# Where the upward projections stand in the fused middle phase of a two-layer transformer kernel

## The chip, the cores and the metric

The kernel runs on one core of a Trainium2 chip, as one program. The metric is the device time of one execution in microseconds (us); for the kernel before it is the median of three runs. One further execution was taken by the hardware profiler, and every row below is from that one.

## The reference

A first block (a gated delta rule beside stick-breaking attention) is followed by a second one. The part that matters here is the end of the first block and the beginning of the second, on 1024 tokens of 1024 features, all in fp32:

```python
# end of the first block
return x + jnp.einsum('bsd,de->bse', merged.astype(x.dtype), w_out)
# beginning of the second block
h = rms_norm(x, attn_norm_g[i])
z = h @ w_in[i]                                   # 1024 x 1952
q  = rms_norm(q_lat,  q_lat_g)  @ w_uq            # z[:, 0:256]   -> 768 columns
kv = rms_norm(kv_lat, kv_lat_g) @ w_ukv           # z[:, 256:384] -> 1024 columns
```

q_lat and kv_lat are the first 384 columns of z. After this come two kinds of attention, which read q, kv and the other columns of z, then an output projection, a gated convolutional feed-forward layer and an embedding gate.

## The kernel before

The kernel is a row of phases. A phase allocates its buffers and semaphores, gives each of five engines its instruction stream, and ends with a barrier over all engines. The changed one is the phase named "trunk", from about 1280 to 1583 us of the span; the phase behind it is "attend".

Each fp32 product is made of three matrix products: every operand is split into a high part and a rest, and high x high, high x rest and rest x high are added in PSUM. So weights are loaded raw from HBM and split: ScalarE copies the raw tile into the high part (`split_hi`, L2943), VectorE subtracts for the rest (`split_lo`, L2948).

`WeightRing` (L2906) does this for the whole phase. Its list of chunks is numbered: 0 and 1 are the two column halves of w_out, 2 to 5 the four column chunks of the second block's w_in (512, 512, 512 and 416 columns), 6 holds w_uq and w_ukv. A chunk has two halves h. There are two slots of split weights (chunk i uses slot i % 2) and one raw buffer per half. One ring step, for chunk i and half h, is: on ScalarE, wait until the half is loaded and until chunk i - 2 has been used to its end (`ended`, L2941), then `split_hi`; on VectorE, `split_lo`; on SP, wait for that `split_lo`, then issue the load of half h of chunk i + 1 (L2935).

The stages of the phase walk over eight token tiles m of 128 tokens each:

- `OutProject` and the `Norm` stages: the output projection of the first block with its residual, the norm, and the turn into feature-major tiles.
- `InProject` (L3254): for each column chunk i and token tile m, 24 products into one PSUM bank (L2987 to L2989), one copy of the bank to an output buffer, one store to HBM (z).
- `LatentScale` and `LatentTurn`: the norm of the 384 latent columns and their turn, spread over the first column chunk and the start of the second.
- `UpProject` (L3432): for each token tile four pieces, q0 and q1 (384 columns, two feature tiles, 6 products each) and kv0 and kv1 (512 columns, one feature tile, 3 products each), at L3488 to L3490, each with its own bank, copy and store (q_mla, kv_mla).

All copies go through `Outputs` (L3218): four output buffers and four PSUM banks, both taken in a fixed rotation in the order of the plan. A copy waits until its bank is filled and until the store of four pieces earlier has landed (`stored`); then it frees the bank. For input tiles ScalarE copies the even m and VectorE the odd ones; for upward pieces ScalarE copies q0 and kv0, VectorE q1 and kv1 (L3239, L3241). SP issues each store when its copy is done (L3246), waiting for the copies one after another.

The order is written out by hand in `trunk_plan` (L3504), a list of stage numbers. Every engine runs the steps of all stages in the order of this list, its own part of each; so a step of SP that waits holds up all stores that stand behind it in the list. In the plan a ring step stands behind the token tiles m = 2 and m = 4 of each of the six chunks; the eight upward steps stand at the very end, with no ring step among them. SP's last work in the phase is the wait for all stores, in the upward stage (`wait_stored`).

Of the kernel before, what the change touches and what calls it, by code (L numbers as in the profile page):

```python
# [17 lines left out]
TT = SEQ // P  # L18
# [5 lines left out]
class Phase:  # L24


    def __init__(self, nc, name):
        self.nc, self.name, self.stack, self.sems = nc, name, ExitStack(), []
# [562 lines left out]
class Heads:  # L591
# [93 lines left out]
    def part(self, tensor, j, s):  # L685
        if 4 * s < self.nh:
            return tensor[:, 4 * s:4 * s + 4, :], 0
        return tensor[:, 4 * s - self.nh:4 * s - self.nh + 4, j % TT * P:(j % TT + 1) * P], 1
# [19 lines left out]
class StickAttention:  # L708
# [34 lines left out]
    def keys(self, u):  # L743
        return (self.units[u][0] + 1) * P
# [9 lines left out]
    def sync(self, sp):  # L754
        def store(j):
            sp.wait_ge(self.o_out, j + 1)
            sp.dma_start(self.out[j * P:(j + 1) * P, :], self.o_sb[:]).then_inc(self.stored, 16)

        self.prep.load(sp, 0)
        self.prep.load_gains(sp)  # L760
        sp.dma_start(self.v_sb[:], self.v.rearrange("(k p) d -> p k d", p=P)).then_inc(self.v_in, 16)
        self.prep.load(sp, 1)
        for i in range(self.steps()):
            if self.next_tile(i, 0) is not None:
                self.prep.load(sp, self.next_tile(i, 0))
            if i >= len(self.units):
                yield
                continue
            j, h = self.units[i]
            if h == 5 and j:  # L770
                store(j - 1)
            yield
        store(TT - 1)
        sp.wait_ge(self.stored, 16 * TT)

    def gpsimd(self, pool):
        self.prep.begin_inverse(pool)
        self.nc.gpsimd.memset(self.zero[:], 0.0).then_inc(self.zeroed, 1)
        for j in range(2):
            self.prep.inverses(pool, j)  # L780
        for i in range(self.steps()):
            if self.next_tile(i, 5) is not None:
                self.prep.inverses(pool, self.next_tile(i, 5))
            yield
# [2198 lines left out]
def token_products(nc, out, hi, lo, tok, ring, i, kt):  # L2983

    for k in range(kt):
        w_hi, w_lo = (w[:, k % (kt // 2)] for w in ring.weights(i, k // (kt // 2)))
        nc.tensor.matmul(out, hi[:, k, tok], w_hi, start=(k == 0), stop=False)  # L2987
        nc.tensor.matmul(out, hi[:, k, tok], w_lo, start=False, stop=False)  # L2988
        last = nc.tensor.matmul(out, lo[:, k, tok], w_hi, start=False, stop=(k == kt - 1))  # L2989
    return last  # L2990


def tile_of(m):
    return slice(m * P, (m + 1) * P)
# [259 lines left out]
class InProject:  # L3254


    def __init__(self, o, outputs, widths, target, first_chunk):
        self.o, self.outputs, self.widths, self.target, self.first_chunk = o, outputs, widths, target, first_chunk
        self.base = [sum(widths[0:i]) for i in range(len(widths))]
        self.latent = None  # L3260
        for i in range(len(widths)):
            o.ring.ended[first_chunk + i] = (o.acc, ("in", i, TT - 1))

    def walk(self):
        return [(i, m) for i in range(len(self.widths)) for m in range(TT)]
# [5 lines left out]
    def sync(self, sp):  # L3271
        for i, m in self.walk():
            self.outputs.store(sp, ("in", i, m), self.target[tile_of(m), self.base[i]:self.base[i] + self.widths[i]], self.widths[i])
            yield

    def gpsimd(self, pool):
        return iter(())
# [16 lines left out]
    def tensor(self, pe):  # L3294
        o = self.o
        for i, m in self.walk():
            key, chunk = ("in", i, m), self.first_chunk + i
            if m == 0:
                for h in range(2):
                    o.ring.wait_split(pe, chunk, h)  # L3300
            if i == 0:
                o.wait_parts(pe, m)
            o.acc.wait_free(pe, key)
            last = token_products(o.nc, o.acc.tile(key)[:, 0:self.widths[i]], o.hi, o.lo, tile_of(m), o.ring, chunk, 8)
            o.acc.fill(last, key)
            yield
# [125 lines left out]
class UpProject:  # L3432
# [4 lines left out]

    def __init__(self, l, q, kv, chunk):
        self.l, self.targets, self.chunk = l, (q, kv), chunk

    def keys(self, m):
        return [("up", m, x) for x in range(len(self.PIECES))]
# [4 lines left out]
    def sync(self, sp):  # L3447
        l = self.l

        def store(m):  # L3450
            for key, (which, c0, w) in zip(self.keys(m), self.PIECES):
                l.outputs.store(sp, key, self.targets[which][tile_of(m), c0:c0 + w], w)

        for m in range(TT):
            store(m)
            yield
        l.outputs.wait_stored(sp)

    def gpsimd(self, pool):
        return iter(())  # L3460
# [34 lines left out]
def take_in_order(plan, stages):  # L3495

    seen = [0] * len(stages)
    for which in plan:
        for slots, key in stages[which].takes(seen[which]):
            slots.take(key)  # L3500
        seen[which] += 1


def trunk_plan():  # L3504

    ring, out, scale, turn, into, l_scale, l_turn, up = range(8)
    plan = [ring, ring]
    for m in range(TT):
        plan += [out, scale]
        plan += [ring] * (m in (2, 4))  # L3510
    for m in range(TT):
        plan += [out]
        plan += [turn] * (m >= 2) + [scale]
        plan += [ring] * (m in (2, 4))
    for i in range(4):
        for m in range(TT):
            if i == 0 and m in (1, 2):
                plan += [turn]
            if 3 <= TT * i + m < 3 + TT:
                plan += [l_turn]  # L3520
            plan += [into]
            if i == 0:
                plan += [l_scale]
            plan += [ring] * (m in (2, 4))
    plan += [up] * TT
    return plan


# [264 lines left out]
def two_blocks(nc, a, out):  # L3793

    def scratch(name, *shape):
        return nc.dram_tensor(f"scratch_{name}", list(shape), F32, kind="Internal").ap()
# [6 lines left out]
    def two_chunks(w0, w1, width):  # L3803

        return lambda c, h: (w0, w1)[h][:, ds(c * width, width)].rearrange("(k p) n -> p k n", p=P)
# [4 lines left out]
    def parts(stack, name, kt):  # L3810
        return (stack.enter_context(nc.sbuf_tensor(f"{name}_hi", [P, kt, SEQ], F32R)),
                stack.enter_context(nc.sbuf_tensor(f"{name}_lo", [P, kt, SEQ], F32R)))

    with ExitStack() as ctx:
# [31 lines left out]
        x1, z2 = scratch("x1", SEQ, D), scratch("z2", SEQ, 1952)  # L3846
        q_mla, kv_mla = scratch("q_mla", SEQ, MLA_H * QK), scratch("kv_mla", SEQ, MLA_H * (NOPE + MLA_V))
        with ExitStack() as stage:
            m_hi, m_lo = parts(stage, "merged", 8)
            with ExitStack() as inner:  # L3850
                hi, lo = parts(inner, "branches", 8)
                gather_branches(nc, "gather1", o_a, o_b, z_a, qkv_z_b[:, 1536:], a["dn_out_gain"], hi, lo, ident)
                project_merge(nc, "merge", hi, lo, two_chunks(a["w_up_a"], a["w_up_b"], 256), gates, m_hi, m_lo)
            with Phase(nc, "trunk") as ph:
                in_widths = [HALF, HALF, HALF, 1952 - 3 * HALF]
                columns_of = [(a["w_out"], 0, HALF), (a["w_out"], HALF, HALF)]
                columns_of += [(a["w_in_2"], i * HALF, w) for i, w in enumerate(in_widths)]
                chunked = [[(4, w, source[h * HALF:(h + 1) * HALF, c0:c0 + w]) for h in range(2)] for source, c0, w in columns_of]
                ring = WeightRing(ph, nc, chunked + [[(2, 768, a["w_uq_2"]), (1, 1024, a["w_ukv_2"])]])
                acc, turn = Slots(ph, "acc", 4, [P, HALF]), Slots(ph, "turn", 1, [P, 8, P])  # L3860
                outputs = Outputs(ph, nc, acc)
                o = OutNorm(ph, nc, m_hi, m_lo, a["x"], x1, a["attn_norm_g_2"], ring, acc, turn, c)
                l = Latent(ph, o, outputs, [a["q_lat_norm_g_2"], a["kv_lat_norm_g_2"]])
                with ExitStack() as own:
                    o.place_inputs(Own(ph, own))
                l.hi, l.lo = (ph.sb(f"latent_{n}", [P, 3, SEQ], F32R) for n in ("hi", "lo"))
                into = InProject(o, outputs, in_widths, z2, 2)
                into.latent = l
                stages = [ring, OutProject(o), NormScale(o), NormTurn(o), into, LatentScale(l), LatentTurn(l),
                          UpProject(l, q_mla, kv_mla, 6)]  # L3870
                plan = trunk_plan()
                take_in_order(plan, stages)
                run_stages(ph, stages, plan)
# [60 lines left out]
```

## Time and profile before

| | us |
|---|---|
| median of 3 runs | 3100.68 (3097.73 to 3104.68) |
| profiled execution | 3099.98 |
| its span | 3097.9 |
| TensorE busy (PE) | 2658.8 (86%) |
| VectorE busy (DVE) | 1276.2 (41%) |
| ScalarE busy (ACT) | 987.7 (32%) |
| mean granted TensorE clock | 0.93 of full speed |

A row of the profile's timeline has the start and the duration in us, the engine, the line of the kernel, the operation and its tiles, and in brackets the idle time before it with what ended that idle time. PE is TensorE, PEld its weight loads, DVE VectorE, ACT ScalarE, POOL GpSimd, SP or SPq the queue that issues the DMAs. The profiled duration of a matrix product is modelled and overlaps the next one, so the pace of TensorE is read from starts. The granted clock is 1.00 at the 2.4 GHz level and 0.50 at the 1.2 GHz level.

### The profile page before, as it was taken

Reading aid. Unit: us, or ns where it says so; the run is one execution under the profiler, and the core shown is the slowest. Engines: PE = TensorE matmul, PEld = TensorE weight load, DVE = VectorE, ACT = ScalarE, POOL = GpSimd, SP = SyncE. Lnnn points to the kernel's source line nnn. Section 1 sums busy time; section 2 is a strip of 40 time slices with the busy share of each in tenths; the row PEclk is TensorE's granted clock in tenths of the full one; section 3 lists DMA queues with packets and bytes.
Section 4 is the critical chain, followed back from the end, with each engine's and each line's share of the span. In section 5 each row is a group of like instructions: output and inputs, shape, how many; then the busy total and the mean of one; then the engine's idle time right before and its main releaser. Section 6 shows DMA issues by size and latency. Waiting matters only on the chain. (4 is left out here: it accounts for less than half of the span.)

```text
span 3097.9 us, 39044 instructions
## 1 busy us (share of the span) xinstructions
PE 2658.8 (86%) x15182; PEld 2295.4 (74%) x15182; DVE 1276.2 (41%) x1831; ACT 987.7 (32%) x1582; POOL 240.3 (8%) x309
## 2 busy tenths in 40 slices
PE   5979999995998928799958889495999999799569
PEld 4859999995887827688946677484888888678469
DVE  4533444433655544342137666513333332333332
ACT  3323222212554531122126666402222221222321
POOL 0002222211000000010013221000000000000000
PEclk9989999997999969899978999797999999899779
DMA  2322212103221133432161110233222221454432
GB/s 89 109 75 77 72 49 59 54 30 99 79 72 38 38 120 136 160 101 94 67 215 48 33 49 16 91 123 103 61 81 61 81 74 55 139 186 142 156 98 93
DMA packets 253786, 272.77 MB, mean 88 GB/s; under 512 B 55716, under 2 KB 190500, under 8 KB 253640
## 3 DMA queue, kind: packets, MB, share of 16 engines
q1 hardware_dynamic: 252584, 268.68, 27.6%
q8 instruction: 98, 1.61, 0.2%
q10 hardware_dynamic: 1056, 2.10, 0.2%
q14 instruction: 48, 0.39, 0.0%
HBM read 193.50 MB, written 77.22 MB: 87 GB/s over the span
## 5 line engine op out<-in xcount | busy, mean ns | idle before, releaser
L395 PE MATMUL ffn_up_acc<-xn_hi,ffn_w_hi 128*128 128x512 f32 x704 | 217.7, 391 | 3.6 <-PEq L39 3.6
L395 PE MATMUL ffn_up_acc<-xn_hi,ffn_w_lo 128*128 128x512 f32 x704 | 217.2, 390 | 0.0
L395 PE MATMUL ffn_up_acc<-xn_lo,ffn_w_hi 128*128 128x512 f32 x704 | 217.2, 390 | 0.0
L1717 PE MATMUL delta_acc<-delta_w_hi,xn_hi 128*128 128x256 f32 x640 | 192.0, 300 | 2.9 <-DVE delta_w_lo L1671 2.9
L1719 PE MATMUL delta_acc<-delta_w_hi,xn_lo 128*128 128x256 f32 x640 | 181.4, 284 | 0.0
L1718 PE MATMUL delta_acc<-delta_w_lo,xn_hi 128*128 128x256 f32 x640 | 181.4, 283 | 0.0
L2987 PE MATMUL trunk_acc<-trunk_ring_hi,merged_hi 128*128 128x512 f32 (+1 forms) x384 | 149.6, 390 | 19.6 <-DVE trunk_ring_lo L2948 19.6
L2107 PE MATMUL ffn_down_acc<-ffn_down_hi 128*128 128x512 f32 x352 | 139.1, 395 | 25.2 <-DVE ffn_down_lo L2092 25.2
L395 PEld LDWEIGHTS ffn_up_acc<-xn_hi,ffn_w_hi 128*128 128x128 f32 x704 | 132.6, 188 | 31.2 <-DMA gather_o<-scratch_o_diff 3.8
L395 PEld LDWEIGHTS ffn_up_acc<-xn_lo,ffn_w_hi 128*128 128x128 f32 x704 | 132.7, 188 | 27.6
L395 PEld LDWEIGHTS ffn_up_acc<-xn_hi,ffn_w_lo 128*128 128x128 f32 x704 | 132.5, 188 | 27.6
L2988 PE MATMUL trunk_acc<-trunk_ring_lo,merged_hi 128*128 128x512 f32 (+1 forms) x384 | 148.0, 385 | 0.0
L2989 PE MATMUL trunk_acc<-trunk_ring_hi,merged_lo 128*128 128x512 f32 (+1 forms) x384 | 147.7, 385 | 0.0
L2092 DVE TENSOR_TENSOR ffn_down_lo<-ffn_down_raw,ffn_down_hi 128x1536 fp32r<-128x1536 f32 x44 | 77.3, 1759 | 165.3 <-ACT ffn_down_hi L2073 165.3
L849 DVE TENSOR_TENSOR_SCAN stick_keep<-stick_keep,stick_zero 128x127 f32<-128x127 f32 (+7 forms) x64 | 86.7, 1355 | 134.8 <-ACT stick_keep L800 134.7
L2108 PE MATMUL ffn_down_acc<-ffn_down_lo,ffn_down_hi 128*128 128x512 f32 x352 | 138.5, 394 | 0.0
L2109 PE MATMUL ffn_down_acc<-ffn_down_hi,ffn_down_lo 128*128 128x512 f32 x352 | 138.4, 393 | 0.0
L1717 PEld LDWEIGHTS delta_acc<-delta_w_hi,xn_hi 128*128 128x128 f32 x640 | 122.4, 191 | 8.9 <-issue 5.5
L2073 ACT ACTIVATE ffn_down_hi<-ffn_down_raw 128x1536 fp32r<-128x1536 f32 x44 | 65.4, 1487 | 189.0 <-PE ffn_down_acc L2109 175.0
L261 PE MATMUL norm_t<-ident,norm_xn 128*128 128x128 f32 x192 | 46.0, 420 | 92.4 <-DVE norm_xn L238 92.4
L1718 PEld LDWEIGHTS delta_acc<-delta_w_lo,xn_hi 128*128 128x128 f32 x640 | 122.5, 191 | 0.0
L1719 PEld LDWEIGHTS delta_acc<-delta_w_hi,xn_lo 128*128 128x128 f32 x640 | 122.3, 191 | 0.0
(401 smaller groups left out, 6294.5 us busy)
## 6 DMA issues: line engine op xcount, KB each, us to landing
ffn_down_raw<-scratch_act_t SPq DMA_DIRECT2D x44, 512.0 KB, 3.5
ffn_w_raw<-in_w_gate SPq DMA_DIRECT2D x22, 512.0 KB, 4.5
ffn_w_raw<-in_w_up SPq DMA_DIRECT2D x22, 512.0 KB, 5.7
scratch_act_t<-ffn_up_silu SPq DMA_DIRECT2D x22, 512.0 KB, 3.2
ffn_down_raw<-in_w_down SPq DMA_DIRECT2D x44, 256.0 KB, 3.7
delta_w_raw<-in_w_in SPq DMA_DIRECT2D x20, 512.0 KB, 3.9
scratch_projected<-delta_out SPq DMA_DIRECT2D x80, 128.0 KB, 1.7
stick_g_raw<-in_w_in SPq DMA_DIRECT2D x16, 512.0 KB, 4.7
```

The costliest lines, as they stand in the source:

```text
L395: last = nc.tensor.matmul(out[:, cols], weight[:, k, ch], part[:, k, cols], start=(k == 0 and first), stop=(k == kt - 1 and weight is w_lo))
L849: nc.vector.tensor_tensor_scan(back, back, self.zero[:].to_broadcast([P, n - 1]), 1.0, ALU.mult, ALU.add).then_inc(self.scanned, 1)
L1717: nc.tensor.matmul(acc, self.hi[:, k, tok], w_hi, start=(k == 0), stop=False, skip_group_check=True)
L1718: nc.tensor.matmul(acc, self.hi[:, k, tok], w_lo, start=False, stop=False, skip_group_check=True)
L1719: last = nc.tensor.matmul(acc, self.lo[:, k, tok], w_hi, start=False, stop=(k == self.kt - 1), skip_group_check=True)
L2092: nc.vector.tensor_tensor(lo[s][:], raw[s][:], hi[s][:].bitcast(F32), ALU.subtract).then_inc(lo_done[s], 1)
L2107: nc.tensor.matmul(acc[m][:], hi[s][:, tok], w_hi, start=start, stop=False, skip_group_check=True)
L2108: nc.tensor.matmul(acc[m][:], hi[s][:, tok], w_lo, start=False, stop=False, skip_group_check=True)
L2109: last = nc.tensor.matmul(acc[m][:], lo[s][:, tok], w_hi, start=False, stop=stop, skip_group_check=True)
L2987: nc.tensor.matmul(out, hi[:, k, tok], w_hi, start=(k == 0), stop=False)
L2988: nc.tensor.matmul(out, hi[:, k, tok], w_lo, start=False, stop=False)
L2989: last = nc.tensor.matmul(out, lo[:, k, tok], w_hi, start=False, stop=(k == kt - 1))
```

## The change

The list of ring chunks gets the upward weights as number 4, between the second and third column chunks, which with the fourth are now 5 and 6. `InProject` takes a list of chunk numbers, [2, 3, 5, 6], in place of the first number, and `UpProject` takes 4 and tells the ring when it has ended. In the plan the eight upward steps stand behind the last token tile of the second column chunk. As the last column chunk now has nothing to split ahead, its two ring steps are gone, and two ring steps stand in the upward stage, behind its token tiles 2 and 4. There they split the third column chunk and load the fourth. The wait for all stores moves to the input stage. The numbers of products, copies, stores and loads are the same.

```diff
@@ class InProject
-    def __init__(self, o, outputs, widths, target, first_chunk):
+    def __init__(self, o, outputs, widths, target, chunks):
...
         for i in range(len(widths)):
-            o.ring.ended[first_chunk + i] = (o.acc, ("in", i, TT - 1))
+            o.ring.ended[chunks[i]] = (o.acc, ("in", i, TT - 1))
...
             self.outputs.store(sp, ("in", i, m), ...
             yield
+        self.outputs.wait_stored(sp)
...
-            key, chunk = ("in", i, m), self.first_chunk + i
+            key, chunk = ("in", i, m), self.chunks[i]
@@ class UpProject
         self.l, self.targets, self.chunk = l, (q, kv), chunk
+        l.o.ring.ended[chunk] = (l.o.acc, self.keys(TT - 1)[-1])
...
-        l.outputs.wait_stored(sp)
@@ trunk_plan
             plan += [into]
             if i == 0:
                 plan += [l_scale]
-            plan += [ring] * (m in (2, 4))
-    plan += [up] * TT
+            plan += [ring] * (m in (2, 4) and i < 3)
+        if i == 1:
+            for m in range(TT):
+                plan += [up] + [ring] * (m in (2, 4))
     return plan
@@ two_blocks
-                ring = WeightRing(ph, nc, chunked + [[(2, 768, a["w_uq_2"]), (1, 1024, a["w_ukv_2"])]])
+                chunked[4:4] = [[(2, 768, a["w_uq_2"]), (1, 1024, a["w_ukv_2"])]]
+                ring = WeightRing(ph, nc, chunked)
...
-                into = InProject(o, outputs, in_widths, z2, 2)
+                into = InProject(o, outputs, in_widths, z2, [2, 3, 5, 6])
...
-                          UpProject(l, q_mla, kv_mla, 6)]
+                          UpProject(l, q_mla, kv_mla, 4)]
```

## Rows read from the trace of the kernel before

**Rows 1.** Busy time by stretch: from:to, its length, then busy us of each engine.
```profile
core 0: us, PE busy (x) PEld busy (x) DVE busy (x) ACT busy (x) POOL busy (x), PEclk, DMA share, GB/s
1424.00:1550.00 126.00, 126.00 (x594) 110.06 (x593) 22.52 (x26) 17.81 (x25) 1.08 (x3) 1.00 0.20 72
1551.00:1579.00 28.00, 27.91 (x143) 25.33 (x141) 9.74 (x17) 8.75 (x16) 0.00 (x0) 1.00 0.67 245
```

**Rows 2.** Timeline of TensorE in the upward stage: start us, duration us, engine, line.
```profile
1550.58 0.34 PE L3488 MATMUL trunk_acc<-trunk_ring_hi,trunk_latent_hi 128*128 128x384 f32 x1
...
1554.11 0.34 PE L3488 MATMUL trunk_acc<-trunk_ring_hi,trunk_latent_hi 128*128 128x384 f32 x1
```

**Rows 3.** Waits in the upward stage: us in total, times, longest.
```profile
ACT trunk_out L3239 <- DMA scratch_kv_mla<-trunk_out: 1.3, 1, 1.3
```

**Rows 4.** Timeline of ScalarE and VectorE in the second column chunk.
```profile
1444.05 0.60 ACT L3239 ACTIVATE trunk_out<-trunk_acc 128x512 f32<-128x512 f32 x1 [5.03 <-PE trunk_acc L2989]
1444.55 1.91 ACT L2943 ACTIVATE trunk_ring_hi<-trunk_ring_raw 128x2048 fp32r<-128x2048 f32 x1
1454.88 0.60 ACT L3239 ACTIVATE trunk_out<-trunk_acc 128x512 f32<-128x512 f32 x1 [8.43 <-PE trunk_acc L2989]
...
1446.49 2.29 DVE L2948 TENSOR_TENSOR trunk_ring_lo<-trunk_ring_raw,trunk_ring_hi 128x2048 fp32r<-128x2048 f32 x1 [6.88 <-ACT trunk_ring_hi L2943]
```

**Rows 5.** DMA issues with us to landing: load, store behind it, upward stores, 1024 KB loads.
```profile
L2935 SPq DMA_DIRECT2D trunk_ring_raw<-in_w_in x1: 383/383/383, 1448.8 to 1448.8; - x1
DMA to landing us min/median/max: 4.8/4.8/4.8
...
L3246 SPq DMA_DIRECT2D scratch_z<-trunk_out x1: 320/320/320, 1450.2 to 1450.2; - x1
DMA to landing us min/median/max: 4.1/4.1/4.1
...
L3246 SPq DMA_DIRECT2D scratch_kv_mla<-trunk_out x8: 319/319/320, 1554.2 to 1565.6; - x8
L3246 SPq DMA_DIRECT2D scratch_q_mla<-trunk_out x8: 319/319/319, 1555.9 to 1567.6; - x8
DMA to landing us min/median/max: 1.8/2.0/2.9
...
trunk_ring_raw<-in_w_in SPq DMA_DIRECT2D x2, 1024.0 KB, 5.7
```

**Rows 6.** Timeline of the copies of the first upward token tile.
```profile
1551.84 0.49 ACT L3239 ACTIVATE trunk_out<-trunk_acc 128x384 f32<-128x384 f32 x1 [5.05 <-PE trunk_acc L3490]
1553.60 0.60 ACT L3239 ACTIVATE trunk_out<-trunk_acc 128x512 f32<-128x512 f32 x1 [1.27 <-PE trunk_acc L3490]
...
1552.90 0.56 DVE L3241 COPY trunk_out<-trunk_acc 128x384 f32<-128x384 f32 x1 [1.53 <-PE trunk_acc L3490]
```

**Rows 7.** Busy time by stretch: TensorE standing still, and the start of the next phase.
```profile
46.00:49.00 3.00, 0.00 (x0) 0.00 (x0) 1.23 (x1) 0.69 (x1) 0.14 (x2) 1.00 0.00 0
1800.00:1802.00 2.00, 0.08 (x1) 0.08 (x2) 1.93 (x10) 0.59 (x2) 0.34 (x1) 1.00 0.19 66
1802.00:1805.00 3.00, 3.00 (x17) 3.00 (x18) 1.39 (x2) 0.98 (x3) 0.00 (x0) 0.57 0.79 203
...
1584.00:1642.00 58.00, 22.71 (x82) 16.68 (x83) 27.08 (x97) 17.58 (x46) 13.55 (x22) 0.50 0.59 169
```

**Rows 8.** Timeline of the end of the phase, with a copy of 416 columns.
```profile
1550.78 0.59 DVE L3241 COPY trunk_out<-trunk_acc 128x416 f32<-128x416 f32 x1 [8.42 <-PE trunk_acc L2989]
...
1578.87 1.11 SPq L3246 DMA_DIRECT2D scratch_kv_mla<-trunk_out  x2
1578.94 0.69 DVE L3241 COPY trunk_out<-trunk_acc 128x512 f32<-128x512 f32 x1 [0.84 <-PE trunk_acc L3490]
...
1582.92 0.34 SPq L2169 DMA_DIRECT2D attend_bias_table<-in_rel_bias  x1
```

More of the change, by code:

```diff
@@ L3254 @@
 class InProject:
-    def __init__(self, o, outputs, widths, target, first_chunk):
-        self.o, self.outputs, self.widths, self.target, self.first_chunk = o, outputs, widths, target, first_chunk
+    def __init__(self, o, outputs, widths, target, chunks):
+        self.o, self.outputs, self.widths, self.target, self.chunks = o, outputs, widths, target, chunks
         self.base = [sum(widths[0:i]) for i in range(len(widths))]
```

## The prediction

> **What bounds the kernel now.** I read the page's shares first, then the stretches of the fused phase one by one, because a share over 3098 us says nothing about one stage. In the stretches [rows 1] the reader is to see that TensorE is busy 126.00 us of 126.00 in the input projection and 27.91 of 28.00 in the upward projection that now ends the phase, at a granted clock of 1.00, while ScalarE and VectorE have 8.75 and 9.74 us of work in the latter. So TensorE's own stream sets the length of both, and an order of the same products gains nothing by itself: there is no idle TensorE time between them for the moved stage to fill. What differs is the rate of the small jobs around the products. An input tile has 24 products, one copy and one store, and takes 5.4 us (ScalarE copies every other one, 10.83 us apart [rows 2]); an upward token tile has 18 products, 12 of them 384 wide, takes 3.53 us (first product at 1550.58, the next token tile's at 1554.11 [rows 3]), and has four copies and four stores. The stage has 8 such tiles: 8 x 3.53 = 28.2 us. Its DMA share is 0.67 at 245 GB/s, against 0.20 at 72 GB/s before it [rows 1]. The upward stage is thus bound by TensorE with the output buffers close behind: one copy already waited 1.3 us for an earlier store [rows 4].
>
> **The change, part by part.** Time t below runs from the first upward product; a piece is one of q0, q1 (384 wide), kv0, kv1 (512 wide). Order of work only: no product, copy, store or load is added or removed.
>
> *Products moved.* Their 28.2 us are spent in the middle instead of at the end. Nil.
>
> *Ring steps that now fall inside the upward stage.* Before, the last ring steps stood in the fourth column chunk, and none in the upward stage. Now the stage's token tiles 2 and 4 are each followed by one: ScalarE splits half of the third column chunk's weights (128x2048, 1.91 us), VectorE makes the rest (2.29 us) [rows 2], and SP, which waits for VectorE there, issues the load of the fourth chunk's half (832 KB). Among the input tiles such a step is free, 24 products (5.4 us) standing for one copy and one store. In the upward stage four pieces pass in 3.53 us. What is queued behind it: on SP the stores of the next token tile, on ScalarE its q0 copy, on VectorE its q1 copy; for the stores wait the copies four pieces later (four output buffers), and for these TensorE (four PSUM banks).
>
> How much later a store behind such a load lands is in the trace: the 832 KB load issued at 1448.8 landed 4.8 us later, at 1453.6, and the 256 KB store issued at 1450.2 took 4.1 us, to 1454.3, so 0.7 us after the load [rows 5]; upward stores without a load ahead take 1.8 to 2.9, median 2.0 [rows 5]. So I take stores as served in order behind the load. The bytes behind it go at 245 GB/s / 0.67 = 366 GB/s [rows 1]: 0.72 us for 256 KB, 0.54 us for 192 KB.
>
> The chain, step by step. The first kv0 copy starts 3.02 us after the stage's first product and takes 0.60 [rows 3, 6]; that of tile 2 ends at t = 7.06 + 3.02 + 0.60 = 10.7. Split 1.91, to 12.6. Rest of the split 2.29, to 14.9. SP issues the load, which lands 4.8 later, at 19.7. Stores of tile 3 behind it: q0 to 20.3, q1 to 20.8, kv0 to 21.5 (0.54, 0.54, 0.72). The kv0 copy of tile 4 needs that last one's buffer: 0.60, to 22.2. On ScalarE the second split follows: 1.91, then 2.29 on VectorE, to 26.4. Second load lands at 31.2; q0 store of tile 5 at 31.8; the q0 copy of tile 6 (0.49) frees its bank at 32.3; TensorE starts tile 7 and ends at 32.3 + 3.53 = 35.9. Without ring steps the end is 28.2, so TensorE stands still for **7.7 us**. In pieces: 0.4 ahead of q1 of tile 4 (its bank waits for a VectorE copy behind the split), 2.9 ahead of tile 5, some 0.2 and 1.3 in tile 6, 2.9 ahead of tile 7.
>
> Bounds of it: if the stores pass the load and land 2.0 after their issue, only the busy VectorE counts. The first VectorE step ends at 14.9 instead of the copy at 13.4 (0.4 of TensorE) and the second at 23.0, its q1 copy to 23.6 where TensorE wanted the bank at 22.5 (1.1): 1.4 us. If each load takes 5.7 us, as the 1024 KB ones of the ring [rows 5], 7.7 + 2 x 0.9 = 9.5 us. I take 7.7, the nearest row being a load of the same size with a store behind it.
>
> The Trainium skill bears on this. In "DMA: Bandwidth & Descriptors", section "Queues, rings and completion order", it says that descriptors are consumed in ring order but that completion is not first-in first-out per issuing engine. By the order of consumption the sum is 7.7 us; by free completion it would go toward 1.4. The one row with a store behind a load sides with order.
>
> *Clock.* TensorE's stops of 2.9 us come twice. The trace has a stop of 3 us with the clock staying at 1.00 (46 to 49 us), and one of 2 us after which it was 0.57 over the next three (1802 to 1805, so 2.6 us of those at half, the 1.2 GHz level) [rows 7]. That is 1.3 us of dense work lost, and the spell may run past 1805: I take 1.8 for a fall. One row each way, so half a chance for each of two stops, 1.8 in all; half of that is hidden, since the spell behind the first stop ends in the second: 0.9 us in the sum, ends 0 and 3.6.
>
> *Weights of the first chunks.* During the first column chunk the ring now loads the upward weights (768 and 512 KB for 1024), and during the second the third chunk's (1024 for 832). One store behind each lands earlier or later by under 1 us, with four buffers of 5.4 us each: nil. A 1024 KB load stands there before too, and TensorE stayed full. If that cover were gone, 0.9 us.
>
> *End of the phase.* The last copy is 0.59 us for 416 columns instead of 0.69 for 512, with a store of 208 KB and none close ahead, instead of 256 KB behind another; VectorE's copy began at 1578.94 and SP's next phase at 1582.92 [rows 8]. I take 0.25 us of gain (0.10 copy, the rest the landing). Bounds 0 and 1.0. Waiting for the stores in the input stage's program instead costs nothing: it is still the last thing SP does.
>
> Sum: 7.7 + 0.9 - 0.25 = 8.35 us. The profiled execution took 3099.98 us (span 3097.9 and 2.1 around it), so 3108.3; against the median 3100.68, 0.7 above that execution, it is 3109.0. **I predict 3109.0 us, 0.27% slower.** A difference under 0.2%, 6.2 us, can't be told from none, so below 3106.9 counts as no change.
>
> **The rivals.**
>
> *B: the stores pass the loads.* Then TensorE stands still for 1.4 us in two pieces, and I put no clock on it: 3100.68 + 1.4 - 0.25 = 3101.8. For it: nothing forces four stores of several buffers to wait as one did. Against it: the 4.1 us [rows 5].
>
> *C: the clock takes long to come back.* If the third to eighth token tiles, 6 x 3.53 = 21.2 us of work, were run half of the time at 1.2 GHz, 10.6 us of work would take 10.6 more, about half of it inside the 7.7 us of stops: +5.3 on the stops, 3100.68 + 7.7 + 5.3 - 0.25 = 3113.4. The Trainium skill ("TensorE: Matmul & The Clock Gate", section "HAM oscillation — how this bites in real kernels") warns of just this shape, dense bursts with a DMA wait between, each burst starting cold. Against it: TensorE is still busy four fifths of the stage, and a whole 3 us stop left the clock up [rows 7].
>
> *D: the other side, faster.* The next phase begins with sparse TensorE work at a granted clock of 0.50 for 58 us, 22.71 of them busy [rows 7]; when the clock rises again depends on when its bursts fall. If the shift of the phase's end brought it up for the last fifth of that busy time, 4.5 us of work at twice the pace save 2.3, and the shorter drain saves up to 1.0. With B's stop: 3100.68 + 1.4 - 1.0 - 2.3 = 3098.8; with no stop at all and half of the busy time at the upper level (11.4 / 2 = 5.7 saved), 3094.0. It decides the sign only where the stores pass the loads. Against it: that stretch mostly waits on other engines.
>
> That the move does what it says but finds nothing to hide is part of the forecast: before, only 0.25 to 1 us lay open at the end.
>
> **How the numbers follow.** Forecast 0.62, its own range 3105 to 3113; B 0.14; C 0.14; D 0.10. Slower by over 0.2%: 0.53 of the forecast's 0.62 and C, 0.67. Within: the forecast's other 0.09, B, and half of D, 0.28. Faster by over 0.2% (below 3094.5): the rest, 0.05. The range takes in B and C: 3101 to 3114.5.
>
> **What would show it.** In the profile after: a weight split of 2048 elements on ScalarE and VectorE among the 384- and 512-wide copies; stores of tiles 3 and 5 landing about 5 us after issue; TensorE idle for about 3 us ahead of tiles 5 and 7 and idle in all 7 to 8 us in the stage, whose length is near 36 us; copies waiting for q and kv stores; the four input chunks as long as before; the end of the phase 7 to 9 us later. I am wrong if those stores land in 2 us, if TensorE's idle time is under 3 us, or if the clock shows 0.5 through most of the stage.

## The result, and the profile after

| | us |
|---|---|
| before, median of 10 runs | 3100.72 |
| after, median of 10 runs | 3112.45 (3105.40 to 3117.64) |
| ratio, 95% interval | 1.0039 (1.0030 to 1.0048) |
| profiled execution after | 3110.97, span 3109.2 |

The change costs 11.7 us (9.3 to 14.9 by the interval); 8.4 were forecast. The direction, the place and the chain were as predicted; the price was higher.

A correction to the reading of the prediction: its numbers for three groups of rows are off. Where it says rows 2 it rests on the group headed Rows 4 (the second column chunk), where it says rows 3 on Rows 2 (TensorE in the upward stage), and where it says rows 4 on Rows 3 (the wait). From here on the numbers are those of the headings.

The stretches of the kernel after, in the form of [rows 1] (the upward stage is 1468.5 to 1507.5):

```profile
core 0: us, PE busy (x) PEld busy (x) DVE busy (x) ACT busy (x) POOL busy (x), PEclk, DMA share, GB/s
1424.00:1468.00 44.00, 44.00 (x200) 36.44 (x199) 8.08 (x11) 6.77 (x13) 1.07 (x3) 1.00 0.28 96
1468.50:1507.50 39.00, 33.17 (x146) 29.72 (x145) 14.31 (x18) 12.09 (x18) 0.00 (x0) 0.87 0.67 223
1486.00:1490.40 4.40, 0.61 (x4) 0.20 (x2) 0.16 (x1) 0.49 (x1) 0.00 (x0) 0.88 1.00 347
1490.40:1499.80 9.40, 9.40 (x35) 8.75 (x36) 4.54 (x5) 3.37 (x4) 0.00 (x0) 0.69 0.62 177
1499.80:1502.30 2.50, 0.46 (x3) 0.06 (x1) 0.16 (x1) 0.49 (x1) 0.00 (x0) 1.00 1.04 388
1507.50:1587.20 79.70, 79.68 (x385) 71.52 (x383) 9.02 (x10) 7.44 (x11) 0.00 (x0) 1.00 0.14 54
```

The reader is to see three things. TensorE is full in the input chunks on both sides, as it was before. In the upward stage it is busy 33.17 of 39.00 us, and in the two holes (1486.0 to 1490.4, 1499.8 to 1502.3) the DMA share is 1.00 and 1.04 (in this measure a full stretch can come out slightly above 1). And the granted clock is 0.87 over the stage; it is low, 0.69, in the busy stretch behind the first hole, where the products take longer.

The first stop, as ScalarE, SP and TensorE have it in the timeline, and then the issues of the load and of the first store behind it with their us to landing:

```profile
1479.05 1.91 ACT L2943 ACTIVATE trunk_ring_hi<-trunk_ring_raw 128x2048 fp32r<-128x2048 f32 x1
1480.85 0.48 ACT L3239 ACTIVATE trunk_out<-trunk_acc 128x384 f32<-128x384 f32 x1
1482.07 0.60 ACT L3239 ACTIVATE trunk_out<-trunk_acc 128x512 f32<-128x512 f32 x1 [0.74 <-PE trunk_acc L3491]
1489.68 0.49 ACT L3239 ACTIVATE trunk_out<-trunk_acc 128x384 f32<-128x384 f32 x1 [7.01 <-DMA scratch_q_mla<-trunk_out]
...
1483.30 0.38 SPq L2935 DMA_DIRECT2D trunk_ring_raw<-in_w_in  x1
1483.73 0.98 SPq L3246 DMA_DIRECT2D scratch_q_mla<-trunk_out  x2
...
1490.32 0.66 PE L3489 MATMUL trunk_acc<-trunk_ring_hi,trunk_latent_hi 128*128 128x384 f32 x1 [3.79 <-ACT trunk_out L3239]
1502.28 0.42 PE L3489 MATMUL trunk_acc<-trunk_ring_hi,trunk_latent_hi 128*128 128x384 f32 x1 [2.04 <-ACT trunk_out L3239]
```
```profile
L2935 SPq DMA_DIRECT2D trunk_ring_raw<-in_w_in x1: 384/384/384, 1483.3 to 1483.3; - x1
DMA to landing us min/median/max: 5.8/5.8/5.8
...
L3246 SPq DMA_DIRECT2D scratch_q_mla<-trunk_out x1: 507/507/507, 1483.7 to 1483.7; - x1
DMA to landing us min/median/max: 5.9/5.9/5.9
```

Read backward: TensorE waited 3.79 us before 1490.32 for the copy at 1489.68, which had waited 7.01 us for a q store, which was issued at 1483.73 right behind the load of 1483.30 and landed at 1489.6, 0.5 us after it. The load took 5.8 us where the row of before had 4.8 [rows 5]; the second one took 5.5. Counted from product start to product start, less the usual pace of 0.23 us, the two stops are 4.0 and 2.2 us; the lengths of stops in the expectations below are of this kind, the numbers in brackets of the rows are the pure idle time (3.79 and 2.04).

The stage by token tile, from the starts of each tile's first product (us from the stage's first product; the last column is the start of the last product):

| | tile 4 | 5 | 6 | 7 | last |
|---|---|---|---|---|---|
| before | 14.09 | 17.61 | 21.13 | 24.65 | 27.93 |
| after | 14.07 | 21.81 | 28.06 | 33.77 | 38.67 |
| added by this step | 0.0 | 4.2 | 2.7 | 2.2 | 1.6 |

Together 10.7 us. The tail of the phase, where before the last copy began at 1578.94 and the next phase at 1582.92 [rows 8]:

```profile
1587.21 0.59 DVE L3241 COPY trunk_out<-trunk_acc 128x416 f32<-128x416 f32 x1 [8.42 <-PE trunk_acc L2989]
1587.83 0.32 SPq L3246 DMA_DIRECT2D scratch_z<-trunk_out  x1
1590.95 0.34 SPq L2169 DMA_DIRECT2D attend_bias_table<-in_rel_bias  x1
```

From the last copy's start to the next phase's first issue it is 3.74 us now and was 3.98, a gain of 0.24. What is left of the difference of the two profiled spans (11.3 us) lies outside the phase: 2.7 less ahead of it and 3.3 more behind it. The part behind it is 1514.98 us before and 1518.25 after, and lies between 1515.4 and 1520.0 in the ten other profiled executions below, whichever kernel it was; no run ties it to the change.

### The profile page after: what moved, and what is told of

It reads as the page before. It is cut to its first block and busy times, and to the rows that moved or that the text cites. A ratio compares the mean times of both kernels' runs of the same rounds, so it can differ in the third digit from the quotient of the medians.

```text
span 3109.2 us, 39044 instructions
## 1 busy us (share of the span) xinstructions
PE 2661.7 (86%) x15182; PEld 2296.8 (74%) x15182; DVE 1276.9 (41%) x1831; ACT 987.4 (32%) x1582; POOL 240.6 (8%) x309
```

## The experiments

Each was timed in five rounds beside the kernel before. "Stage" is the time from the first to the start of the last upward product in the one profiled execution: 27.9 us before, 38.7 after.

**1. The loads later.** A stage of its own issues the two loads of the fourth chunk at the start of the third.

```diff
-            if i + 1 < len(self.chunks):
+            if i + 1 < len(self.chunks) and i != 5:
                 self.load(sp, i + 1, h)
...
+            plan += [8] * (i == 2 and m < 2)      # LateLoads(ring, 6): ring.load(sp, 6, h)
             plan += [into]
```

> The changed kernel, with the two loads of the fourth column chunk issued at the start of the third column chunk; the two weight splits stay in the upward stage. Theory (stores queue behind the loads): TensorE's stops of 4.0 and 2.2 us and both clock falls go, 0.4 and 0.9 us remain for the busy VectorE; the upward stage falls from 39.0 us to 29.4 and the time to about 3102. Rival (the splits themselves hold up the copies): the stage stays near 37 us or more, the time at 3110 to 3112. Rival (the changed order costs in another place): stage shorter, but the time stays above 3108.

Measured: 3100.56 us, ratio 0.9998 (0.9989 to 1.0007); stage 29.5 us. Its stretch:

```profile
1469.40:1499.10 29.70, 28.96 (x145) 25.76 (x144) 14.12 (x18) 12.08 (x18) 0.00 (x0) 1.00 0.64 232
```

Both splits are still there (ACT 12.08 and DVE 14.12 us, as after), the clock is 1.00, and 9.2 of the 10.7 us are gone. The loads' place among the upward stores is the cause, and the changed order alone costs nothing that can be measured.

**2. The same cost at the old place.** The kernel before, with the two ring steps added to its last stage.

```diff
-    plan += [up] * TT
+    for m in range(TT):
+        plan += [up] + [8] * (m in (2, 4))        # Extra: split raw[h] again, then load 832 KB into it
```

> The kernel before, its upward stage still last, with two added ring steps in it (behind its token tiles 2 and 4): each splits 2048 elements per partition again and then loads 832 KB into the raw buffer, results unused. Theory (it is the ring steps among the upward pieces that cost, not the place of the stage): the stage takes 37 to 40 us for 28.1, time 3109 to 3113. Rival (the place costs): the time stays within 2 us of 3100.7.

Measured: 3112.31 us, ratio 1.0042 (1.0030 to 1.0054); stage 38.4 us, tile steps of 4.0, 1.3, 3.7 and 1.5 us. The stage at its old place loses what it lost at the new one. The rival, the place itself, is out.

**3. Only the loads, twice.**

```diff
 # Extra.sync, behind the upward token tiles 2 and 4; no splits
+    sp.dma_start(r.raw[h][:, 0:4 * 416]..., self.source[h]...).then_inc(r.loaded[h], 16)
```

> The kernel before with the two added 832 KB loads in the upward stage (behind token tiles 2 and 4), and no added splits, so that SP has nothing to wait for ahead of them; loaded data unused. Theory (a chain of split, load and store): the load starts some 3 us earlier than behind a split, and with landings of 4.8 to 5.8 us the stops are 1.5 to 3.5 us in all, time 3102 to 3105. Rival (the load alone is the whole cost): 8 to 11 us, 3109 or more. Rival (the load costs nothing without the split): 3100.7.

Measured: 3108.89 us (5 runs), ratio 1.0033 (1.0020 to 1.0046), yet a stage of 32.4 us, 4.5 more than before. The time missed the expectation and the trace nearly met it, so the kernel was run again.

> The same kernel as the one with only the two added loads in the upward stage of the kernel before, again, because its time lay 9.6 us over the kernel before while its trace shows the stage only 4.5 us longer. If the trace is right and the five times were high by chance: 3103 to 3106 and a stage of 32 to 33 us. If the loads cost something outside the stage: 3108 to 3110 again, with the stage at 32 to 33 us. If the profiled execution was a lucky one: 3108 to 3110, and a stage of 35 us or more.

Measured: 3106.05 us (11 runs), ratio 1.0017 (1.0008 to 1.0026); stage 36.7 us. None of the three outcomes came whole: the time is that of the first, the stage that of the third. The stretches of the two executions, first run and repeat:

```profile
1546.90:1579.50 32.60, 28.79 (x145) 25.52 (x144) 9.90 (x16) 8.37 (x16) 0.00 (x0) 1.00 0.76 258
```
```profile
1548.30:1585.30 37.00, 31.69 (x146) 28.05 (x144) 9.90 (x16) 8.70 (x16) 0.00 (x0) 0.91 0.71 237
```

And the second load of each, first run and repeat (issue row, then landing):

```profile
L3509 SPq DMA_DIRECT2D trunk_ring_raw<-in_w_in x1: 434/434/434, 1568.8 to 1568.8; - x1
DMA to landing us min/median/max: 5.9/5.9/5.9
```
```profile
L3509 SPq DMA_DIRECT2D trunk_ring_raw<-in_w_in x1: 433/433/433, 1570.6 to 1570.6; - x1
DMA to landing us min/median/max: 7.2/7.2/7.2
```

The first load took 5.8 us in one execution and 5.9 in the other, the second 5.9 and 7.2. With the longer one came an idle time of 4.04 us ahead of tile 7 in place of 1.74, and behind it the clock fell to the 1.2 GHz level: the last tile took 6.1 us there and 3.4 in the first run. So the stage differs between executions of the same program by 4.3 us, of which 2.8 are this slow last tile, and the first profiled execution was the cheaper one. Loads without splits cost 4.4 to 9.6 us by the medians: more than the 1.5 to 3.5 of the expectation. How much of the 4.4 to 9.6 is chance of five runs stays open. A difference of stages between two kernels with one profiled execution each has this spread too.

**4. Only the splits.**

```diff
 # Extra, behind the upward token tiles 2 and 4; no loads
+    r.nc.scalar.activation(r.hi[1][:, h], r.raw[h][:], ACT.Copy).then_inc(r.hi_done[h], 1)
+    r.nc.vector.tensor_tensor(r.lo[1][:, h], r.raw[h][:], r.hi[1][:, h].bitcast(F32), ALU.subtract ...
```

> The kernel before with the two added splits in the upward stage and no added loads; results unused. Theory: only the busy VectorE holds TensorE, 1.2 us in all, time about 3102, no clock fall. Rival (the splits are the main cost): 5 us or more, 3106 and up.

Measured: 3099.73 us, ratio 1.0003 (0.9994 to 1.0013); stage 29.7 us, 1.8 more than before:

```profile
1544.00:1573.90 29.90, 28.95 (x146) 25.59 (x144) 14.02 (x18) 12.02 (x18) 0.00 (x0) 1.00 0.62 228
```

The splits alone are not the cost. With a load behind them they also move it: SP waits for VectorE and issues the load 3 us later, right ahead of the next tile's stores (at 14.8 us of the stage in experiment 2 and in the changed kernel, at 11.9 in experiment 3). Whether this shift costs anything is not shown. Against the 10.5 us that loads and splits together add to the stage, the splits alone (1.8) and the loads alone (4.5 in the first run, 8.8 in the repeat) add up to 6.3 or to 10.6.

**5. Half the bytes.**

```diff
+        if i == 6:      # only two of the four feature tiles are loaded
+            sp.dma_start(...[:, 0:2], source[0:2 * P]...).then_inc(self.loaded[h], 16)
```

> The changed kernel, with each of the fourth column chunk's two loads cut to half its bytes (416 KB for 832; the other half of that chunk's weights is left out, so its columns are computed from stale weights). Theory (each stop is as long as the load ahead of the stores; a load with stores behind it lands after 5.5 to 6 us, not 4.8, which is the step that the prediction sized too small): with landings of 3.3 to 3.6 us the stops ahead of token tiles 5 and 7 shrink from 3.85 us to 1.4 to 1.7 each, TensorE's stage is 32.6 to 33.3 us for 39.0, time about 3105 to 3106. Rival (one fixed delay per load whatever its size): the stage stays at 37 us or more, 3110 to 3112.

Measured: 3104.97 us, ratio 1.0010 (1.0001 to 1.0019); stage 33.6 us. The first load:

```profile
L2936 SPq DMA_DIRECT2D trunk_ring_raw<-in_w_in x1: 384/384/384, 1482.0 to 1482.0; - x1
DMA to landing us min/median/max: 3.8/3.8/3.8
```

It landed 2.0 us sooner than the full one, and tile 5 started at 19.84 us of the stage instead of 21.81, 2.0 us sooner. At this stop the gain is as long as the load is shorter. Both waits of SP for VectorE are still there, and 5.1 of the 10.7 us are gone, so they are not the main cost.

**6. The same bytes in eight pieces.**

```diff
-            if i + 1 < len(self.chunks):
+            if i + 1 < len(self.chunks) and i != 5:
                 self.load(sp, i + 1, h)
...
+            # LateLoads: four loads of 208 KB for each half, one behind each token tile's stores
+            sp.dma_start(into[:, q], source[q * P:(q + 1) * P]).then_inc(r.loaded[h], 16)
```

> The changed kernel with each of the two 832 KB loads cut into four of 208 KB, one behind the stores of each token tile from 2 on (the last two at the start of the third column chunk); splits stay, SP still waits for VectorE ahead of each half's first piece. Theory (a store waits for the bytes ahead of it): stores land within 3 us of issue, TensorE stops 1.5 to 3 us in all, no clock fall, stage 30 to 31 us, time 3102 to 3104. Rival (SP's wait for VectorE is what counts): the stops stay at 5 us or more, 3108 and up.

Measured: 3101.03 us, ratio 1.0004 (0.9996 to 1.0013); stage 31.0 us, clock 1.00:

```profile
1468.80:1500.00 31.20, 29.12 (x145) 25.66 (x144) 14.20 (x18) 11.49 (x17) 0.00 (x0) 1.00 0.69 241
```

SP's first wait for VectorE is as before, with the first piece issued at 14.8 us of the stage. Its second is in effect gone, as the second half's first piece stands only behind token tile 6; experiment 5, which has both, covers this. The bytes are the same but for two pieces, and the stores beside them landed within 1.9 to 3.9 us of their issue. 7.7 of the 10.7 us are gone.

**7. Another queue.** The two loads are issued by GpSimd, on its own queue.

```diff
+    def gpsimd(self, pool):                       # WeightRing, for i == 5
+        pool.wait_ge(self.lo_done[h], i + 1)
+        pool.dma_start(...).then_inc(self.pool_loaded[h], 16)
...
-            if i + 1 < len(self.chunks):
+            if i + 1 < len(self.chunks) and i != 5:      # SP's part: no load of chunk 6
```

> The changed kernel with the two loads of the fourth column chunk issued by GpSimd on its own queue, so that SP's stores neither wait for the split nor stand behind the load in one queue; the bytes share the same DMA engines at the same time. Theory A (order in the queue is what holds the stores): stores of token tiles 3 and 5 land in 3 us or less, stage 29 to 31 us, time about 3103. Theory B (the DMA engines are full, whatever the queue): the stores beside the load still take 4 to 6 us; as they are issued earlier the stage is 32 to 35 us, time 3105 to 3108.

Measured: 3108.33 us (6 runs), ratio 1.0030 (1.0018 to 1.0042); stage 35.3 us. The DMA issues from 1460 to 1515 us (KB each, median us to landing), the stores of token tile 3 beside the load (kv0, kv1), then the first of tile 4:

```profile
trunk_ring_raw<-in_w_in POOLq DMA_DIRECT2D x2, 832.0 KB, 7.4
```
```profile
L3253 SPq DMA_DIRECT2D scratch_kv_mla<-trunk_out x2: 432/437/442, 1483.3 to 1483.8; - x2
DMA to landing us min/median/max: 3.1/5.2/7.3
...
L3253 SPq DMA_DIRECT2D scratch_q_mla<-trunk_out x1: 323/323/323, 1484.6 to 1484.6; - x1
DMA to landing us min/median/max: 6.9/6.9/6.9
```

Stores on SP's queue still took up to 7.3 us with no load ahead of them there, and in each microsecond from 1484 to 1491 the DMA share was 0.90 or more. Theory B holds in kind (stage and time came out 0.3 us above its ranges): the 16 DMA engines are full while the load runs, whichever queue it came from. The stage was 3.4 us shorter than in the changed kernel, which is within what two executions of one program differed by in experiment 3, and the intervals of the times overlap (1.0018 to 1.0042 here, 1.0030 to 1.0048 there), so a gain by the other queue is not shown. Two things changed with it, which this run does not part: SP no longer waits for VectorE, and the load shares the engines with the stores (8.1 and 6.6 us for the two loads instead of 5.8 and 5.5).

**8. Six output buffers.**

```diff
 class Outputs:
-    N = 4
+    N = 6
```

> The changed kernel with six output buffers in place of four; the loads stay. Theory: the copies wait for stores six pieces back, two pieces (some 1.4 to 2.1 us) later, so the stops shrink but do not go: 6.4 us in all by the chain against 9.5 by the same chain with four, stage 34.5 to 37 us with the clock, time about 3108. Rival (four PSUM banks, not the output buffers, are the limit): no difference, 3112. Rival (the buffers alone are to blame): no stops, 3102.

Measured: 3105.29 us, ratio 1.0018 (1.0009 to 1.0027); stage 34.5 us. The stops shrank and did not go, as the chain has it; the buffers are one link of it. The time fell 2.7 us further than expected; the stage is at the lower end of its range.

**9. The clock held up.** Idle products fill TensorE's stops.

```diff
+                for _ in range({5: 17, 7: 9}.get(m, 0) if key[2] == 0 else 0):
+                    l.o.nc.tensor.matmul(l.junk[:], l.hi[:, 2, tile_of(0)], ..., start=True, stop=True)
                 l.o.acc.wait_free(pe, key)
```

> The changed kernel with 17 idle products ahead of the upward stage's token tile 5 and 9 ahead of tile 7, into a bank that nobody reads, so that TensorE works through most of its two stops. Theory (the clock falls come from the stops and cost 4.6 us of the 10.8): the granted clock stays at 1.00 in the stage, the stage is 1.5 to 4 us shorter than the changed kernel's 39.0 (part of the saved time turns into a longer second stop, since the store sets it), time about 3109.5. Rival (the stops alone cost all of it, the slow spells are hidden in them): same length within 0.5 us, or longer by what the idle products overrun.

Measured: 3111.34 us (6 runs), ratio 1.0041 (1.0029 to 1.0053); stage 38.6 us. Its stretch, and that of experiment 2:

```profile
1465.70:1504.50 38.80, 35.72 (x171) 30.40 (x170) 14.21 (x18) 11.65 (x18) 0.00 (x0) 1.00 0.65 218
```
```profile
1544.80:1583.40 38.60, 30.52 (x145) 26.89 (x143) 14.21 (x18) 12.06 (x18) 0.00 (x0) 0.96 0.66 222
```

The granted clock stayed at 1.00 and the stage was as long as the changed kernel's at 0.87, so my account of 4.6 us for the clock fell and the rival came true. In this execution the q1 store of tile 3 took 7.4 us (tile 5 began at 21.98), which by my estimate hides up to about 1 us of gain. The comparison of steps says the same: with the slow spell right behind the first stop (changed kernel) the starts of tiles 6 and 7 move by 2.7 + 2.2 = 4.9 us, without it (experiment 2) by 1.3 + 3.7 = 5.0. The first spell is swallowed by the second stop, as far as one execution of each shows. Behind the last stop nothing swallows it: 1.6 and 1.5 us there at the 1.2 GHz level, 0.1 in the kernel with idle products.

## Why the prediction was right, and where its sizes were off

*TensorE has no idle time for the stage to fill.* Right: it was full in all input chunks before and after, and experiment 1, the same order without the loads among the pieces, is at 0.9998.

*A store behind the load waits for it.* Right, and this is nearly the whole cost (9.2 of the stage's 10.7 us go in experiment 1): experiments 1, 5 and 6 take it away in three ways, in whole or in part, and the time goes with it; experiment 2 puts it into the kernel before and gets 11.8 us. One word of it has to be changed. The prediction took the order in the queue as the mechanism. Experiment 7 shows that the full DMA engines hold the stores even on another queue; whether order in one queue makes it any worse is not shown. So rival B would not have come true on two queues either. On the page's rule (the Trainium skill, "DMA: Bandwidth & Descriptors", section "Issuing engines are not separate DMA queues": DMAs of several issuing engines run on the same 16 and interleave) the trace agrees: 7.3 us for a store with no load in its queue.

*The chain, 7.7 us.* This is the mis-sized term. Its load of 4.8 us was read where one store followed 1.4 us behind [rows 5]; with four stores right behind, the load took 5.8 and 5.5 us in the changed kernel, and 5.5 to 7.2 in the experiments that keep it whole, on SP's queue and among the pieces. The stage grew by 10.7 us; less the 1.6 of the clock this is 9.1, against 7.7 + 1.0 + 0.7 = 9.4 by the chain with the landings as measured. The upper bound that the prediction had put beside it, 9.5 us for loads of 5.7, was the better value. The row was right in bytes and wrong in company. That it is the company which made the load longer is my reading; no run times the same load in this place with one store behind it.

*The pieces of it.* Forecast 0.4 + 2.9 for tile 5, 1.5 for tile 6, 2.9 for tile 7; in experiment 2, where little of the clock is in it, 4.0, 1.3 and 3.7. Bound 1.4 us for the splits alone: 1.8 measured in the stage.

*The clock, 0.9 us.* Two falls came, one behind each stop, where one was expected. The first cost nothing, the second 1.6. The term was thus taken at about half of what the one fall behind the last stop cost, and that cost is itself a matter of the execution: 1.5 us in experiment 2, 2.8 in the repeat of experiment 3. Rival C (slow for half of the stage's work) did not come: 0.87 over the stage.

*The signs.* The stores of tiles 3 and 5 landed 5.9 and 5.6 us after issue, for about 5. TensorE was idle 3.79 us ahead of tile 5, but only 2.04 ahead of tile 7 and 5.8 in all, for 7 to 8: the work at the 1.2 GHz level behind the first stop filled part of the second. In experiment 2, where the clock stayed up behind the first stop, the idle time is 38.60 - 30.52 = 8.1 us. The stage is 39.0 us long, for near 36.

*The end of the phase, 0.25 us.* Measured 0.24. *Weights of the first chunks, nil.* From the phase's first product to the end of the second column chunk it took 0.2 us longer in this one execution, which is nothing to build on.

*Rival D, faster.* The next phase begins with the same 58 us at 0.50, shifted with the phase, with the same TensorE work in it as in [rows 7]:

```profile
1591.80:1649.80 58.00, 22.71 (x82) 16.70 (x83) 27.11 (x97) 17.56 (x46) 13.76 (x23) 0.50 0.60 169
```

Nothing was won there.

*The sum.* 8.35 us forecast, 11.7 measured (9.3 to 14.9), of which the profiled phase shows 10.7 - 0.24 and 0.2. The remaining 1 us is inside the interval.

## What to carry to other kernels

Before a stage is moved, look at what its new neighbours put into the DMA engines and at how many pieces its output buffers reach ahead: the same 1.7 MB of weights were free among tiles that store once in 5.4 us and cost some 9 us among tiles that store four times in 3.5 us. Where a large load must stand there, cut it into pieces of the size of the stores, or put it behind the stage; more buffers give back only a part, and another queue no more than that. And take the duration of a transfer from a row with the same traffic around it, not only of the same size: 4.8 us here with one store behind, 5.5 to 7.2 with four.

## What was not expected of the hardware

The landing of one and the same load (832 KB, stores behind it) varied from 5.5 to 7.2 us between executions; the stage of one and the same program varied by 4.3 us, 2.8 of them by the clock. On GpSimd's queue, with the stores on SP's, the load took 8.1 and 6.6 us.

Stops of TensorE of some 2 to 4 us were followed by a fall to the 1.2 GHz level in some cases and not in others, and not by their length: both stops of the changed kernel were (idle 3.79 and 2.04 us), of the two longest in experiment 2 (3.54 and 3.43 us) only the second, and in experiment 5 a stop of 1.82 us was (granted clock 0.50 from 1489 to 1491 us), while the next one of 1.55 us was not.
